# A hybrid decoder block on eight cores: norm sums of later first-FFN tiles placed behind their transfer, and a rebuilt last tile

## The chip, the cores and the metric

The kernel runs on the 8 cores of one Trainium2 chip. Each core computes one sequence of the batch, and no core talks to another. The time of a run is that of the slowest core, in microseconds (us). A profile is one further execution, recorded on every core; "the trace" below is that of core 7, the slowest, unless another core is named.

## The reference, cut to what matters

```python
def ada_rmsnorm(x, g, shift, scale):
    return rmsnorm(x, g) * (1.0 + scale[:, None, :]) + shift[:, None, :]
...
c_act = jax.nn.silu(c)
mod = c_act @ w_mod[l] + b_mod[l]                 # nine vectors of 1024
h = ada_rmsnorm(x, g_ffn1[l], sh1, sc1)
x = x + 0.5 * gt1[:, None, :] * swiglu_ffn(h, w_ffn1_in[l], w_ffn1_out[l])
h = ada_rmsnorm(x, g_mix[l], sh2, sc2)
...                                               # conv group and RG-LRU group, both from h @ w_in
x = x + gt2[:, None, :] * y_mix
h = ada_rmsnorm(x, g_ffn2[l], sh3, sc3)
x = x + 0.5 * gt3[:, None, :] * swiglu_ffn(h, w_ffn2_in[l], w_ffn2_out[l])
return ada_rmsnorm(x, g_final, f_shift, f_scale)
```

`x` is (8, 4096, 1024) in float32, the FFN's hidden width is 2816. Per core that is a first FFN, a mixer and a second FFN over 4096 tokens, with a norm over the 1024 channels ahead of each and one at the end.

## The kernel before

**Tiles.** The 4096 tokens are 8 tiles of 512. A tile of `x` lies in SBUF as 8 chunks (`fc` 0 to 7) of 128 channels x 512 tokens, so each channel sum of a norm runs across chunks and partitions: ScalarE squares a chunk, VectorE adds it to a running sum (`accum`), and after the eighth chunk one matmul with a matrix of ones (`total`) sums over the partitions into a PSUM bank. `rstd_ops` then takes Ln and Exp on ScalarE, and `apply` scales the chunks to bf16 in one of three buffers `hbs` (`sb_hb`). The running sum is `sb_rstdm`, the squares `sb_ntmp`, the last sum in bf16 `sb_sqb`; the final norm has its own, `sb_rstdo`, `sb_sqo`, `sb_sqbo`.

**Jobs.** `f_gen` runs the two FFNs over a ring of five weight slabs (`fslots`, `sb_fs`, 512 KB each), 33 slabs per job: 22 for the input matrix, 11 for the output matrix. The jobs are the first FFN of the pairs (2,3), (4,5), (0,1), then of tile 6, then the second FFN of 0 and 1, the first FFN of 7 and the second of 2 to 7. A slab of a pair feeds 32 matmuls, of a single tile 16. The next slab of the ring is asked for when one is free again. From tile 6 on the mixer of a tile (`r_gen`, `c_gen`, `mb_gen`) runs beside an FFN job. In the first jobs the float32 weights are also cast to bf16 copies in memory, and the modulation vectors are computed on VectorE from streamed `wmod`.

**Tiles of x.** There are four slots `xs` for tiles; slot 3 becomes mixer buffers after the pairs. `xl_gen` loads a tile of the input by eight transfers of 256 KB (`xload`, on POOL's queue). They share one semaphore, and `xload` gives every chunk the count and the planned time of the last one, so that whoever reads a chunk waits for the whole tile. `lx_gen` loads tiles 2 to 7 again from scratch memory for the mixer. A slot whose tile was written to `y` is loaded again with the next tile.

**The order of the work.** Nothing is ordered on the chip but by each engine's queue and its semaphores. The program is written out ahead: `run_streams` takes generators ("streams"), each of which yields an operation with a planned cost, and always emits the operation that could start first in planned time. Transfers have a planned landing time too, from a rate and a latency (`DMA_RATE`, `DMA_LAT`). Each engine then runs its list strictly in order. An operation that planned time puts ahead of a transfer's real landing therefore holds up everything behind it on its engine. `n1_gen` is the stream of the norms ahead of the first FFN. It takes an `hbs` buffer and the lock of the norm's buffers, and then yields the squares.

**The end of a tile.** `o_gen` does the final norm. It squares the chunks as the second FFN's output matmuls finish them (`x3c` flags), sums, then per chunk one VectorE multiply, one ScalarE Identity with the shift, and a 256 KB store to `y` on POOL's queue. Chunk `fc` of every tile uses semaphore `s_y[fc]`. After its last instruction POOL waits for all of them.

Every DMA, activation and vector operation is recorded by a helper, so rows name few lines: L417 the DMAs, L434 ScalarE, L437 and L441 VectorE, L457 matmuls.

## Time and profile before

| | |
|---|---|
| median of 3 runs | 2374.32 us (2369.19 to 2564.76) |
| the profiled execution, its own time | 2375.25 us |
| its span on core 7 (first to last instruction) | 2373.7 us |
| spans of all cores | 2348.4 to 2373.7 us |
| TensorE (PE) busy | 2249.8 us, 95% |
| VectorE (DVE) / ScalarE (ACT) / GpSimd (POOL) busy | 56% / 40% / 12% |
| granted TensorE clock, mean | 0.988 |

Times in rows are microseconds from the span's start. A row of a timeline has a start, a duration, the engine, the line, the operation, what it writes and reads, its count, and in brackets how long the engine was idle before it and what ended that. Rows of waits have the sum, the number and the longest. PEclk is the clock granted to TensorE, as a share of its 2.4 GHz. SPq and POOLq are the queues that issue transfers.

### The profile page before, as it was taken

How to read it: one execution, taken by the hardware profiler on the slowest of the kernel's cores; microseconds unless marked ns; L12 is line 12 of the kernel's file. 1: busy time of each engine (PE TensorE's matmuls, PEld its weight loads, DVE VectorE, ACT ScalarE, POOL GpSimd, SP SyncE). 2: the span in 40 equal slices, each digit the busy share in tenths (PEclk: the TensorE clock that was granted, in tenths of full speed). 3: DMA queues.
4: the chain of work that ended last, by engine and by line, in shares of the span. 5: the costliest groups of instructions: out<-in, count | busy, mean ns of one | idle time of the engine just before them, and what ended most of it. 6: DMA issues, size and time to landing. Idle time of an engine off the chain costs nothing.

```text
span 2373.7 us, 34088 instructions; the slowest of 8 cores (2348.4 to 2373.7 us)
## 1 busy us (share of the span) xinstructions
PE 2249.8 (95%) x10864; PEld 1006.1 (42%) x10864; DVE 1324.7 (56%) x2131; ACT 956.6 (40%) x1473; POOL 287.0 (12%) x552
## 2 busy tenths in 40 slices
PE   1999998998999899899999999999999999999995
PEld 0444443443444344344444444444444444444442
DVE  5323225524433485674776476487487588477522
ACT  3313213303110533553565536436536556454512
POOL 0011110020000110201110120111111111120000
PEclk9999999999999999999999999999999999999998
DMA  9899798899866685654665665556456566564452
GB/s 258 189 232 215 194 206 214 214 212 243 214 187 164 191 223 170 190 167 141 194 207 158 207 200 191 154 171 227 153 178 214 160 171 222 158 186 138 151 177 89
DMA packets 122704, 446.86 MB, mean 188 GB/s; under 512 B 18864, under 2 KB 19248, under 8 KB 121520
## 3 DMA queue, kind: packets, MB, share of 16 engines
q1 hardware_dynamic: 90864, 330.44, 44.7%
q0 software_dynamic: 31664, 114.23, 21.5%
q8 instruction: 91, 1.49, 0.3%
q14 instruction: 85, 0.70, 0.1%
HBM read 426.87 MB, written 71.30 MB: 210 GB/s over the span
## 4 chain that ended last, share of the span: by engine, by line
PE 85%; DMA 8%; issue 2%; DVE 2%; ACT 2%; POOL 1%; SPq 0%; DVEq 0%; ACTq 0%; POOLq 0%
PE ps L457 83%; DMA sb_x<-x 2%; PE ps L1097 2%; DMA sb_cs<-wmod 2%; DMA sb_fs<-b 1%; DMA sb_fs<-w 1%; DMA sb_hidB<-wmod 1%; DMA sb_cs<-bm 1%; DVE sb_rstdm L441 1%; DMA x<-sb_x 0%; SPq L417 0%; POOL sb_urep L1087 0%; ACT sb_hb L434 0%; POOL sb_x L417 0%; ACT sb_ntmp L434 0%
## 5 line engine op out<-in xcount | busy, mean ns | idle before, releaser
L457 PE MATMUL ps<-sb_hb,sb_fs 128*128 128x512 bf16 x5632 | 1245.6, 382 | 35.5 <-DMA sb_fs<-w 14.2
L457 PEld LDWEIGHTS ps<-sb_hb,sb_fs 128*128 128x128 bf16 x5632 | 553.9, 98 | 711.8 <-issue 62.5
L457 PE MATMUL ps<-sb_hidA,sb_fs 128*128 128x512 bf16 x2288 | 505.7, 379 | 0.8 <-DVE sb_hidA L441 0.8
L434 ACT ACTIVATE sb_sgf<-ps 128x512 f32<-128x512 f32 x352 | 206.5, 593 | 406.8 <-PE ps L457 364.3
L457 PEld LDWEIGHTS ps<-sb_hidA,sb_fs 128*128 128x128 bf16 x2288 | 223.9, 98 | 269.6 <-issue 1.3
L441 DVE TENSOR_TENSOR sb_hidA<-ps,sb_sgf 128x512 bf16<-128x512 f32 x286 | 195.4, 688 | 227.1 <-PE ps L457 161.4
L457 PE MATMUL ps<-sb_hb,sb_cs 128*128 128x512 bf16 x992 | 224.2, 379 | 4.5 <-DMA sb_cs<-bm 3.4
L1087 POOL DMA_DIRECT2D sb_urep<-sb_ub x256 | 131.0, 520 | 694.5 <-PE ps L457 435.6
L437 DVE SCALAR_TENSOR_TENSOR sb_x<-ps,sb_gth,sb_x 128x512 f32<-128x512 f32 x128 | 96.0, 750 | 174.8 <-PE ps L457 174.4
L434 ACT ACT_TABLE_LOAD x102 | 130.9, 1283 | 154.4 <-PE ps L457 134.1
L437 DVE SCALAR_TENSOR_TENSOR sb_ux<-sb_ub,sb_vecs,sb_ux 128x512 f32<-128x512 bf16 x240 | 179.7, 749 | 10.0 <-DVE sb_ux L437 0.9
L434 ACT ACTIVATE sb_ntmp<-sb_x 128x512 f32<-128x512 f32 x168 | 103.6, 627 | 197.7 <-DVE sb_x L437 110.7
L441 DVE TENSOR_TENSOR sb_rstdm<-sb_rstdm,sb_ntmp 128x512 f32<-128x512 f32 x144 | 99.3, 689 | 131.5 <-ACT sb_ntmp L434 127.5
L437 DVE SCALAR_TENSOR_TENSOR sb_ntmp<-sb_x,sb_gs,sb_rstdm 128x512 f32<-128x512 f32 x192 | 137.8, 748 | 50.0 <-ACT sb_rstdm L434 41.7
L434 ACT ACTIVATE sb_hb<-sb_ntmp,sb_modv 128x512 bf16<-128x512 f32 x192 | 133.1, 720 | 43.1 <-DVE sb_ntmp L437 42.7
L457 PEld LDWEIGHTS ps<-sb_hb,sb_cs 128*128 128x128 bf16 x992 | 96.5, 98 | 122.3 <-issue 7.6
L457 PE MATMUL ps<-sb_hb,sb_rs 128*128 128x512 bf16 x544 | 128.8, 381 | 0.6 <-DVE sb_gy L437 0.4
L457 PE MATMUL ps<-sb_hidB,sb_fs 128*128 128x512 bf16 x528 | 117.9, 379 | 0.0
L441 DVE TENSOR_TENSOR sb_hidB<-ps,sb_sgf 128x512 bf16<-128x512 f32 x66 | 45.6, 691 | 109.5 <-PE ps L457 106.0
L417 POOL DMA_DIRECT2D y<-sb_x x64 | 35.0, 547 | 521.3 <-ACT sb_sgf L434 198.0
L437 DVE SCALAR_TENSOR_TENSOR sb_x<-ps,sb_modv,sb_x 128x512 f32<-128x512 f32 x64 | 47.9, 749 | 74.4 <-PE ps L457 74.3
L457 PEld LDWEIGHTS ps<-sb_hb,sb_rs 128*128 128x128 bf16 x544 | 53.4, 99 | 66.7 <-issue 4.1
(104 smaller groups left out, 1338.6 us busy)
## 6 DMA issues: line engine op xcount, KB each, us to landing
sb_fs<-b SPq DMA_DIRECT2D x396, 512.0 KB, 4.4
sb_cs<-bm SPq DMA_DIRECT2D x78, 512.0 KB, 4.1
sb_x<-x POOLq DMA_DIRECT2D x96, 256.0 KB, 7.9
sb_cs<-wmod SPq DMA_DIRECT2D x46, 512.0 KB, 12.6
sb_rs<-bm SPq DMA_DIRECT2D x34, 512.0 KB, 5.0
sb_fs<-w POOLq DMA_DIRECT2D x33, 512.0 KB, 9.9
b<-sb_fs SPq DMA_DIRECT2D x33, 512.0 KB, 8.8
b<-w POOLq DMA_DIRECT2D x33, 512.0 KB, 10.3
```

What stands on the lines that cost most here:

```text
L417: return Op(eng, lambda h: [h.dma_start(out=out_ap, in_=in_ap)], reads, writes, dma=sem, nbytes=nbytes)
L434: return Op(ACT, lambda h: [h.activation(out=out, in_=in_, func=func, **kw)], reads, writes, cost, tset)
L437: return Op(DVE, lambda h: [h.scalar_tensor_tensor(out=out, in0=in0, scalar=scalar, in1=in1, op0=op0, op1=op1)], reads, writes, cost)
L441: return Op(DVE, lambda h: [h.tensor_tensor(out=out, in0=in0, in1=in1, op=op)], reads, writes, cost)
L457: out.append(h.matmul(ps[:, bank, :], lhsT=l, rhs=r, start=(first and k == 0), stop=(last and k == n - 1)))
L1087: out.append(h.dma_start(out=urep[q][32 * sft:32 * sft + 32, 1 - h2:2, :], in_=ub[32 * q:32 * q + 32, 1 + h2:2 * h2 + 2, sft:sft + WU]))
L1097: out.append(h.matmul(ps[32 * q:32 * q + 32, b, :], lhsT=sl[:, 8 * (c % 2) + r, 32 * q:32 * q + 32], rhs=urep[q][:, c % 2, 4 * r:4 * r + T ...
```

## The change

- **A planner condition for the norms of later first-FFN tiles.** `n1_gen` yields `landed(si, margin)` for every group but the first: the stream goes on once PE's planned clock is `margin` past the planned landing of the tile, 30 us for tiles 4, 5, 0 and 1, 12 us for 6 and 7. It stands ahead of the taking of `normlock`, behind that of the `hbs` buffer. It adds no instruction and no wait; it moves the norm's instructions in the lists. Should no stream have anything to emit, `core.force` lets all such conditions pass once.
- **Semaphores of the stores.** `s_y` is now one of four by tile (`t % 4`), shared by the tile's eight stores, and after the loop every chunk of the slot is marked with the full count. A later load into the slot waits for that.
- **The last tile** (`last`): the PSUM bank is taken at its start. Ahead of chunk 7's flag the ones matmul over the sum of chunks 0 to 6 is emitted (it opens the accumulation), and an Exp of one column (`hstate` into `sgm`), which brings the table load with it. Chunk 7's square is written as bf16 into `cvb` and summed by a second ones matmul into the same bank, in place of the last VectorE add. Its eight stores go from SyncE (`SP`) on a semaphore of their own, `s_yl`.
- **A renaming of the conv code** by the constants `CVD` and `CVP` (`spread`, `v_gen`, `c_gen`, the layout of `vecs`). With the values given it yields the same operations with the same operands.

```diff
@@ Core, run_streams
-        self.now = 0.0
+        self.force = False
...
-        assert best is not None, [s.name for s in streams]
+        if best is None:
+            assert not core.force, [s.name for s in streams]
+            core.force = True
+            continue
+        core.force = False
@@ semaphores
-        s_y = [newsem(f"s_y{k}") for k in range(8)]
+        s_y = [newsem(f"s_y{k}") for k in range(4)]
+        s_yl = newsem("s_yl")
@@ accum
-        def accum(st, src, r_src):
+        def accum(st, src, r_src, split=False):
...
+            if split and k == 7:
+                yield act(cvb[:], src, AF.Square, [r_src], [r_cvb])
+                return
             q = nxt(name, 2)
             yield act(sq[q][:], src, AF.Square, [r_src], [r_sq[q]])
-            if k < 7:
+            if split and k == 6:
+                yield add(accb[:], acc[:], sq[q][:], [r_sq[q], r_acc], [r_accb])
+            elif k < 7:
                 yield add(acc[:], acc[:], sq[q][:], [r_sq[q]], [r_acc])
@@ n1_gen
+        def landed(si, margin):
+            return lambda: core.force or PE.clock > max([r.tw for r in r_x[si]]) + margin
...
-                    yield lambda: normlock.take(1)
                     if first:
                         yield lambda: mused[0] >= 5
+                    elif gi > 0:
+                        yield landed(si, 30.0 if gi < 3 else 12.0)
+                    yield lambda: normlock.take(1)
@@ o_gen
-                yield from stats(xt, r_xt, st, before=lambda fc, t=t: flag(("x3c", t, fc)))
-                got = yield lambda: bankM.take(1)
-                bank = got[0]
-                yield total(st, bank)
+                last = t == n_tiles - 1
+                if last:
+                    got = yield lambda: bankM.take(1)
+                    bank = got[0]
+                    for fc in range(8):
+                        if fc == 7:
+                            yield mm(bank, [(ones_bf[:], sqbo[:])], [r_sqbo, r_ones], last=False)
+                            yield act(sgm[:, 0:1], hstate[:, 0:1], AF.Exp, [r_hst[0]], [r_sgm], tset="E", cost=0.2)
+                        yield flag(("x3c", t, fc))
+                        yield from accum(st, xt[:, fc, :], r_xt[fc], True)
+                    yield mm(bank, [(ones_bf[:], cvb[:])], [r_cvb, r_ones], first=False)
+                else:
+                    (the four lines removed above)
...
-                    yield dma(PL, y_d[t, fc], xt[:, fc, :], [r_xt[fc]], [], s_y[fc], MB // 4)
+                    sy = s_y[t % 4] if not last else s_yl
+                    yield dma(SP if last else PL, y_d[t, fc], xt[:, fc, :], [r_xt[fc]], [], sy, MB // 4)
+                for fc in range(8):
+                    r_xt[fc].r[sy] = sy.val
                 xpool.give(si)
```

POOL's final wait covers `s_y` and `s_yl`.

## Rows read from the trace of the kernel before

**Rows 1.** The page: the span, and busy time by engine.

```profile
span 2373.7 us, 34088 instructions; the slowest of 8 cores (2348.4 to 2373.7 us)
...
PE 2249.8 (95%) x10864; PEld 1006.1 (42%) x10864; DVE 1324.7 (56%) x2131; ACT 956.6 (40%) x1473; POOL 287.0 (12%) x552
```

**Rows 2.** Waits of PE over the whole span: total, times, longest.

```profile
PE ps L457 <- DVE sb_sqb L441: 56.1, 9, 33.0
```

**Rows 3.** Timeline of PE around the ones matmuls of tiles 0 and 6.

```profile
365.48 0.58 PE L457 MATMUL ps<-sb_sqb,sb_ones 128*128 128x512 bf16 x1 [5.96 <-DVE sb_sqb L441]
365.86 14.33 PE L457 MATMUL ps<-sb_hb,sb_fs 128*128 128x512 bf16 x55
...
540.61 22.57 PE L457 MATMUL ps<-sb_hb,sb_fs 128*128 128x512 bf16 x96 [2.87 <-DMA sb_fs<-b]
569.30 0.59 PE L457 MATMUL ps<-sb_sqb,sb_ones 128*128 128x512 bf16 x1 [6.13 <-DVE sb_sqb L441]
569.68 10.49 PE L457 MATMUL ps<-sb_hb,sb_fs 128*128 128x512 bf16 x35
```

**Rows 4.** Timeline of ACT: the first squares of tiles 0 and 6.

```profile
356.15 0.63 ACT L434 ACTIVATE sb_rstdm<-sb_x 128x512 f32<-128x512 f32 x1 [11.37 <-DMA sb_x<-x]
...
559.50 0.63 ACT L434 ACTIVATE sb_rstdm<-sb_x 128x512 f32<-128x512 f32 x1 [7.61 <-DMA sb_x<-x]
```

**Rows 5.** Stretches: length, busy PE, PEld, DVE, ACT, POOL (instructions), PEclk, DMA share, GB/s.

```profile
360.00:370.00 10.00, 4.52 (x11) 1.61 (x12) 6.96 (x13) 6.39 (x9) 0.00 (x0) 0.68 0.87 272
...
440.00:500.00 60.00, 60.00 (x279) 27.20 (x278) 26.22 (x40) 13.81 (x21) 7.51 (x14) 1.00 0.82 188
...
570.00:580.00 10.00, 10.00 (x35) 4.00 (x34) 7.06 (x12) 9.05 (x13) 0.00 (x0) 0.74 0.73 143
```

**Rows 6.** Slabs asked for at 530.92 and at 549.45: KB, us to landing.

```profile
sb_fs<-b SPq DMA_DIRECT2D x1, 512.0 KB, 34.2
...
sb_fs<-b SPq DMA_DIRECT2D x1, 512.0 KB, 30.7
```

**Rows 7.** Waits of PE on core 4, 340 to 600 us.

```profile
PE ps L457 <- DVE sb_sqb L441: 13.2, 2, 10.1
```

**Rows 8.** Timeline of PE: the ones matmul of tile 7's first norm.

```profile
1218.37 0.38 PE L457 MATMUL ps<-sb_sqb,sb_ones 128*128 128x512 bf16 x1 [1.02 <-DVE sb_ub L449]
```

**Rows 9.** Timeline of ACT: tile 5's first square, and the instruction after its norm.

```profile
232.40 0.63 ACT L434 ACTIVATE sb_rstdm<-sb_x 128x512 f32<-128x512 f32 x1 [22.57 <-DMA sb_x<-x]
...
288.80 1.28 ACT L434 ACT_TABLE_LOAD   x1 [34.67 <-PE ps L457]
```

**Rows 10.** Loads behind stores: waits for `y` by line, then the refill at 1642 us.

```profile
  POOL sb_x L417: 4.9, 4
...
1641.96 3.76 POOL L417 DMA_DIRECT2D sb_x<-x  x7
1647.38 0.54 POOL L417 DMA_DIRECT2D sb_x<-x  x1 [1.65 <-DMA y<-sb_x]
...
1656.26 0.63 ACT L434 ACTIVATE sb_rstdm<-sb_x 128x512 f32<-128x512 f32 x1 [2.37 <-DMA sb_x<-x]
```

**Rows 11.** Timeline of the last tile's final norm.

```profile
2350.75 0.69 DVE L441 TENSOR_TENSOR sb_sqbo<-sb_rstdo,sb_sqo 128x512 bf16<-128x512 f32 x1 [0.95 <-ACT sb_sqo L434]
...
2351.59 0.38 PE L457 MATMUL ps<-sb_sqbo,sb_ones 128*128 128x512 bf16 x1 [2.65 <-DVE sb_sqbo L441]
2352.10 1.28 ACT L434 ACT_TABLE_LOAD   x1 [1.52 <-PE ps L457]
...
2356.94 5.18 POOL L417 DMA_DIRECT2D y<-sb_x  x8 [99.19 <-ACT sb_x L434]
```

**Rows 12.** The stretch behind the last store, columns as in rows 5.

```profile
2365.00:2373.70 8.70, 0.00 (x0) 0.00 (x0) 0.00 (x0) 0.00 (x0) 0.00 (x0) 0.50 0.00 0
```

**Rows 13.** Timeline of ACT: a mixer's Exp and Ln operations behind one table load.

```profile
1014.71 1.28 ACT L434 ACT_TABLE_LOAD   x1
...
1018.85 2.18 ACT L434 ACTIVATE sb_mbuf<-sb_mbuf 128x512 f32<-128x512 f32 x4
```

More of the change, by code:

```diff
@@ L24 @@
 WU = 540
+CVD = (0,)
+CVP = (1, 2, 3)
 V_G1, V_GM, V_G2, V_GF = 0, 8, 16, 24
@@ L1082, in spread @@
         def spread(h2):
+            c0 = max(2 * h2, CVP[0])
             def fn(h):
@@ L1086, in fn @@
                     for sft in range(4):
-                        out.append(h.dma_start(out=urep[q][32 * sft:32 * sft + 32, 1 - h2:2, :],
-                                               in_=ub[32 * q:32 * q + 32, 1 + h2:2 * h2 + 2, sft:sft + WU]))
+                        out.append(h.dma_start(out=urep[q][32 * sft:32 * sft + 32, c0 - 2 * h2:2, :],
+                                               in_=ub[32 * q:32 * q + 32, c0:2 * h2 + 2, sft:sft + WU]))
                 return out
-            return Op(PL, fn, [r_ub[2 * h2 + k] for k in range(1 - h2, 2)], [r_urep], dma=s_ur, nbytes=128 * 4 * (1 + h2) * WU * 2, ndma=16)
+            return Op(PL, fn, [r_ub[k] for k in range(c0, 2 * h2 + 2)], [r_urep], dma=s_ur, nbytes=128 * 4 * (2 * h2 + 2 - c0) * WU * 2, ndma=16)
         def conv_mm(b, sl, r_sl, c):
@@ L1127, in c_gen @@
                 bankM.give(bv)
-                if c == 0:
-                    streams.append(Stream(f"V{i}", v_gen(i), dict(b_m, dve=0)))
-                if c == 1:
+                if c in CVD:
+                    streams.append(Stream(f"V{i}.{c}", v_gen(i, c), b_v))
+                if c == 1 and CVP[0] < 2:
                     yield spread(0)
             flags.add(("glu", i))
-            for c in range(1, 4):
+            for c in CVP:
+                if c == 2 and CVP[0] == 2:
+                    yield cring.has(k0 + 4)
+                    cring.done(k0 + 4)
+                    yield spread(1)
                 k = k0 + 4 + c // 2
@@ L1149, in c_gen @@
             cx = [ux[:, c, 3:3 + T] for c in range(4)]
-            yield act(varb[:], cx[1], AF.Square, [r_ux[1]], [r_var])
-            for c in (2, 3, 0):
-                if c == 2:
-                    yield add(meanb[:], cx[1], cx[2], [r_ux[1], r_ux[2]], [r_mean])
-                elif c == 3:
-                    yield add(meanb[:], meanb[:], cx[3], [r_ux[3]], [r_mean])
-                else:
-                    yield flag(("cv", i))
-                    yield add(cvb[:], meanb[:], cx[0], [r_ux[0], r_mean], [r_cvb])
+            lo = CVP + CVD
+            for n, c in enumerate(lo):
+                if c in CVD:
+                    yield flag(("cv", i, c))
+                if n == 0:
+                    yield act(varb[:], cx[c], AF.Square, [r_ux[c]], [r_var])
+                    continue
+                if n == 1:
+                    yield add(meanb[:], cx[lo[0]], cx[c], [r_ux[lo[0]], r_ux[c]], [r_mean])
+                elif n == 2:
+                    yield add(meanb[:], meanb[:], cx[c], [r_ux[c]], [r_mean])
+                else:
+                    yield add(cvb[:], meanb[:], cx[c], [r_ux[c], r_mean], [r_cvb])
                 yield act(sgm[:], cx[c], AF.Square, [r_ux[c]], [r_sgm])
-                if c > 0:
+                if n < 3:
                     yield add(varb[:], varb[:], sgm[:], [r_sgm], [r_var])
@@ L1273, in o_gen @@
                 st = stat_o()
-                yield from stats(xt, r_xt, st, before=lambda fc, t=t: flag(("x3c", t, fc)))
-                got = yield lambda: bankM.take(1)
-                bank = got[0]
-                yield total(st, bank)
+                last = t == n_tiles - 1
[10 more added lines that the diff above has]
+                else:
+                    yield from stats(xt, r_xt, st, before=lambda fc, t=t: flag(("x3c", t, fc)))
+                    got = yield lambda: bankM.take(1)
+                    bank = got[0]
+                    yield total(st, bank)
                 yield rstd_ops(rstd_o, r_ro, bank, 1.0 / D)
@@ L1316, in build_program @@
         build_program.model = {e.name: (round(e.clock, 1), round(e.busy, 1)) for e in (PE, ACT, DVE, SP, PL)}
-        final_vals = [(sm.h, sm.val) for sm in s_y]
+        final_vals = [(sm.h, sm.val) for sm in s_y + [s_yl]]
         with nc.Block() as block:
@@ L1367, in prep_inputs @@
             shared[:, V_RCW + 4 * cc + k] = rcw[k, cc * 128:(cc + 1) * 128]
-    shared[:, V_CW:V_CW + NCONV] = f(inputs["conv_w"][0])[:, 0:128].T
+    for j, cc in enumerate(CVD):
+        shared[:, V_CW + NCONV * j:V_CW + NCONV * (j + 1)] = f(inputs["conv_w"][0])[:, 128 * cc:128 * cc + 128].T
     def blocks(w, rows, cols):
```

20 lines of the change are left out of this document (11 added, 9 removed).

## Prediction

> **What bounds the kernel now.** I read the page first, then the waits of PE, then its timeline. PE is busy for 2249.8 of 2373.7 us, every other engine for at most 56% [rows 1]. So time is gained only where PE stands still, or behind its last matmul. The waits of PE say where it stands: 56.1 us in 9 waits are for `sb_sqb`, the last sum of a norm, that is, for a ones matmul which sits in PE's queue ahead of its data [rows 2]. The longest, 33.0 us, is the kernel's start, which the change does not touch. Of the rest, the timeline shows two large ones, 5.96 us at tile 0's norm and 6.13 us at tile 6's [rows 3]; the other 11.0 us are spread over six. The reader should follow each one step back. ACT stood for 11.37 and 7.61 us at the tile's first square, waiting for the transfer of `x` [rows 4]. The squares start when the tile lands, at 356.15 and 559.50; eight squares and seven adds later the sum is there, about 9 us on. PE had arrived at its ones matmul at 359.5 and 563.2. The planner had the tile land earlier than it did.
>
> **What a stall costs.** It is more than its idle time. Behind the first, 55 matmuls take 14.33 us [rows 3]; at the full clock they take 0.215 us each (60.00 us for 279 in [rows 5]), 11.83 in all. The granted clock of that stretch is 0.68, so part of it ran at 1.2 instead of 2.4 GHz [rows 5]. That is 2.5 us more, and the first stall costs 5.96 + 2.50 = 8.5 us. Behind the second, 35 matmuls take 10.49 us in place of 7.53, at a granted clock of 0.74 [rows 3, 5]: 6.13 + 2.96 = 9.1 us.
>
> **The norms moved back.** Nothing is added; the squares, adds, ones matmul, Ln, Exp and the 16 operations of `apply` go later in three queues. The first stall: PE came 6 us early, the margin is 30. It goes whole, 8.5 us. Nothing is late next: the pair (4,5) began at about 287 us (its first Silu stands behind ACT's table load at 288.80 [rows 9]) and takes 33 slabs of 32 x 0.215 = 6.9 us, so tile 0 is wanted from about 515 on. Does the gain survive until then? The weights must come as much earlier. Between 440 and 500 us the DMA engines are busy for a share of 0.82 [rows 5], so 0.18 x 60 = 11 us are spare, more than 8.5. I keep it all.
>
> The second stall: PE was 6 us early, the margin is 12, so the sum is ready first. But here the weights come next. PE had just done 96 matmuls, three slabs of the pair, behind a wait of 2.87 us for a slab [rows 3], so slabs come with nothing to spare. The one it takes next was asked for at 530.92 and took 34.2 us [rows 6]: it landed at 565.1, and 1.9 us of the stall stay. The slab two further on was asked for at 549.45 and took 30.7 us, landing at 580.15; with 6.9 us for a pair's slab (32 x 0.215) PE wants it at 565.1 + 13.8 = 578.9 and waits 1.2 us more. From then on PE is at 580.15 where it was 64 matmuls behind 569.68: 35 in 10.49 us, 29 more in 6.2, at 586.4. The gain is 6.2 us, between 3.5 (if these slabs get no sooner and a clock drop follows their wait) and 9.1 (if the transfers move up with PE).
>
> Tiles 4 and 1 show no wait of PE and give nothing. Tile 5's squares started at 232.40, its norm left ACT at 288.80 - 34.67 = 254.1, and ACT's next work comes at 288.8 [rows 9]. Thirty us later it ends at 284.1, so 4.7 us of cover are left; without them tile 4 alone could run up to the ring's five slabs ahead, 17 us. Nothing. Tile 7's ones matmul comes 1.02 us late [rows 8]: 1.0 us gained, between 0 and 2.
>
> **The stores' semaphores.** Before, a load into a freed slot waited for its own chunk's store. At 1641.96 POOL issued seven of the eight loads while the last store was still under way, and only the eighth waited, until 1647.38 [rows 10]. After the change all eight wait, so the last is issued 7 x 0.54 = 3.8 us later, and what stands behind them on POOL's queue (the 16 transfers of a `urep` spread, the stores of `y`, tile writes) is as late at most. Such waits for `y` occur four times [rows 10]. How much later does the tile land? Nothing, if the eight loads are limited by their 2 MB (the last one took until 1656.26, 8.9 us behind its issue); 3.8 us, if by their issue. I take the middle, 1.9. One of the four is tile 7's first load, where the margin of 12 us covers it. At 1656.26 ACT already waits 2.37 us for the tile [rows 10], so the 1.9 us may reach PE there. For the other two, which no large wait of PE marks (they are among the six that share 11.0 us), I take 0.6 together. Loss 2.5 us, between 0 and 8 (3.8 at two of them).
>
> **The last tile.** The last VectorE add goes. Its row starts at 2350.75 and the ones matmul at 2351.59 [rows 11], 0.84 us; the second ones matmul starts as soon as the square is there. The table load of 1.28 us stands between that matmul and Ln [rows 11]; moved ahead, it lies beside PE's last eight matmuls (8 x 0.215 = 1.7 us), for which chunk 7's square waits anyway. The stores: ACT is done at 2361.0, POOL's last issue starts 0.54 before 2362.12, at 2361.58 [rows 11], since POOL spends 0.54 to 0.66 us on each. SyncE has nothing else to do then: 0.5 us, perhaps 0.7 with a shorter way to the data, between 0 and 1.3. The added ones matmul costs 0.2 us of PE ahead of the end, the Exp of one column nothing. Together 0.84 + 1.28 + 0.7 = 2.8 us, between 1.9 and 3.4.
>
> The Trainium skill's page "ScalarE: Activation LUTs" (section "What ACT_TABLE_LOAD costs") gives about 2.66 us for a switch of tables, load and drain together. By it the last tile would save 1.4 us more. The trace doesn't agree: the instruction behind the load starts 1.29 us after the load did.
>
> **Sum.** 8.5 + 6.2 + 1.0 + 2.8 - 2.5 = 16.0 us. The profiled execution took 2375.25 us (span 2373.7 and 1.5 around it), so 2359.2 us; it lies 0.9 above the median of the runs shown. I predict **2358 us**. Other cores have the same stalls; core 4 loses 13.2 us in two of them [rows 7], so the slowest core should gain about as much as core 7.
>
> **Rivals.**
> - *The transfers become the bound.* PE's wait for a slab at 540.6 (2.87 us, [rows 3]) grows by what the first stall gave: the queue that took 34.2 us for a slab [rows 6] is no faster. Then 8.5 us are given back at about 540 us: gain 7.5, **2367 us**. For it: landing times of over 30 us. Against: the spare 11 us at 440 to 500 us. Chance 0.17.
> - *A new order brings new waits.* The planner rebuilds every queue from the first moved norm on, and what waits remain (the 11.0 us in six for `sb_sqb` among them, [rows 2, 3]) falls by chance. Two new ones of 8 us undo the change: **2374 us**. The trace can't price this. Chance 0.13.
> - *The other side: refills.* Each of the four refills is 3.8 us late and drops the clock for 2.5 us as the stalls did, 25.2 in all, against 18.5 gained: **2381 us**. It decides from 4.6 us per refill. Against: tile 7's is covered, and at the one in [rows 10] PE lost no more than its share of 11.0 us though the tile was 2.37 us late for ACT. Chance 0.05.
> - *The condition is too weak for tile 6.* It counts in planned time. Core 4's longest stall is 10.1 us [rows 7], the margin 12. If the tile comes 4 us later still, the second gain is lost: **2364 us**. Chance 0.05.
> - *The end shrinks.* For 8.7 us behind the last store no engine works and nothing moves [rows 12]. If that is POOL's closing of its own transfers, it could fall away with stores on SyncE: **2350 us**. But POOL still waits for the stores and has issued transfers all along. Chance 0.07.
> - *The table load stays.* If an Exp ahead brings a table without Ln, a second load follows: 1.3 us more, **2360 us**. Against: in the mixer one load covers four Exp, two Ln and two Exp, with the Exp first [rows 13]. Chance 0.02. The Trainium skill's page "ScalarE: Activation LUTs" (section "Table sets: the hidden batching unit") lists a set for Exp that lacks Ln beside one that has both; by that rule the load would stay if the first were picked.
>
> **How the numbers follow.** The forecast has the other 0.51. Forecast, too-weak condition, staying load, transfers and shrinking end hold 0.82; with the bounds of the small terms that is 2349 to 2369 us. The measurement can tell about 2%, here 47 us, from no change. No case reaches that on either side: faster 0.02, within 2% 0.96, slower 0.02, the two for what I have not thought of.
>
> **What would show it.** Right: no wait of PE over 1 us at the ones matmuls of tiles 0 and 6, and the granted clock 1.00 behind them; a slab wait of 1 to 3 us at about 555 us; the eight loads of a refill in one run behind the last store's landing; at the end no table load between ones matmul and Ln, and the last store issued 0.1 us behind the last Identity; 8.7 us of quiet at the end as before. Wrong: waits for slabs of over 8 us more than before, ones matmuls that wait in the mixer part, or a tile 4/5 job that starts with one tile only.

## The result, and the profile after

The changed kernel is slightly slower. Over 20 runs each its median is 2398.91 us against 2378.72 us; the ratio is 1.0067, with a 95% interval of 1.0047 to 1.0087, so about 16 us were lost (11 to 21) where 16 were forecast as a gain. (The medians count every run; the ratios, here and below, leave out the disturbed ones.) The profiled execution took 2381.32 us, the quickest of its 20; before it was 2375.25 us.

The page of the changed kernel, to be held against [rows 1]:

```profile
span 2379.7 us, 34056 instructions; the slowest of 8 cores (2365.9 to 2379.7 us)
PE 2253.4 (95%) x10865; PEld 1007.1 (42%) x10865; DVE 1322.6 (56%) x2130; ACT 953.5 (40%) x1472; POOL 282.8 (12%) x544
```

The work is the same to one matmul, and PE is no less the bound. So the loss, like the hoped-for gain, lies in PE's waits. Its waits over the whole span on core 1, which answer to [rows 2]:

```profile
PE ps L464 <- DVE sb_sqb L448: 63.4, 9, 32.3
```

The start still holds 32.3 us; the other eight waits for a norm's sum add up to 31.1 us on this core, where on core 7, the slowest of the kernel before, they were 23.1. (All helper lines moved by seven: L457 is now L464, L441 is L448, L434 is L441, L417 is L424.)

**Where tile 0's norm waits now.** The timeline of core 1 around it (start, length, engine, line, operation, in brackets the idle time ahead and what ended it):

```profile
374.71 1.22 DVE L663 SCALAR_TENSOR_TENSOR sb_junk<-sb_cs,sb_cb 128x1024 bf16<-128x1024 f32 x1 [7.01 <-DMA sb_cs<-wmod]
...
376.64 0.60 ACT L441 ACTIVATE sb_sgf<-ps 128x512 f32<-128x512 f32 x1 [8.25 <-DVE sb_hidA L448]
377.13 0.62 ACT L441 ACTIVATE sb_rstdm<-sb_x 128x512 f32<-128x512 f32 x1
...
385.71 1.22 DVE L663 SCALAR_TENSOR_TENSOR sb_junk<-sb_cs,sb_cb 128x1024 bf16<-128x1024 f32 x1 [8.57 <-DMA sb_cs<-wmod]
...
387.47 2.27 DVE L448 TENSOR_TENSOR sb_rstdm<-sb_rstdm,sb_ntmp 128x512 f32<-128x512 f32 x3
388.24 0.63 ACT L441 ACTIVATE sb_ntmp<-sb_x 128x512 f32<-128x512 f32 x1 [8.96 <-DVE sb_rstdm L448]
...
393.57 0.59 PE L464 MATMUL ps<-sb_sqb,sb_ones 128*128 128x512 bf16 x1 [13.06 <-DVE sb_sqb L448]
```

Read the lines in order of time. ACT's first square, at 377.13, waits for nothing any more: the tile has long landed, and the 11.37 us of [rows 4] are gone. But VectorE, which must add the squares, stands in its own queue at a product of the modulation, the multiply of a `wmod` slab (`sb_junk`, L663). Two such slabs are late: VectorE stands 7.01 and 8.57 us for them. The adds stand behind them, ACT's squares behind the adds, and PE's ones matmul comes 13.06 us late, where it had been 5.96 [rows 3]. This is not peculiar to core 1: on core 7, the slowest of the kernel before, it is 8.28 us.

The stretch of the stall and the one behind it, on core 1, columns as in [rows 5]:

```profile
380.00:390.00 10.00, 0.52 (x3) 0.02 (x1) 4.08 (x7) 1.43 (x3) 0.00 (x0) 0.77 0.98 311
390.00:400.00 10.00, 6.42 (x18) 2.43 (x19) 7.25 (x12) 7.78 (x11) 0.00 (x0) 0.55 0.23 90
```

In the second stretch the granted clock is 0.55, nearly the lower level of 1.2 GHz throughout. While PE stood, the DMA engines were busy for a share of 0.98; behind the stall it is 0.23. So the transfers already asked for ran on beside the stall, and then few were under way. That new ones waited for buffers that PE and VectorE had to free would explain it; no run tests that.

Tile 6's stall shrank on five of the eight cores and grew on three. On core 7 it was 6.13 us [rows 3] and is 1.47, on core 1 it is 2.43; the mean over the cores went from 6.1 to 4.2. On core 5 it went from 4.94 to 10.76 us, by the same mechanism as at tile 0:

```profile
555.62 0.63 ACT L441 ACTIVATE sb_rstdm<-sb_x 128x512 f32<-128x512 f32 x1 [3.46 <-DMA sb_x<-x]
563.65 1.23 DVE L663 SCALAR_TENSOR_TENSOR sb_junk<-sb_cs,sb_cb 128x1024 bf16<-128x1024 f32 x1 [11.40 <-DMA sb_cs<-wmod]
571.11 0.59 PE L464 MATMUL ps<-sb_sqb,sb_ones 128*128 128x512 bf16 x1 [10.76 <-DVE sb_sqb L448]
```

Here ACT still waits for the tile too, 3.46 us (1.3 to 3.5 us on four cores), so the 12 us of planned margin are not always enough.

**Where a refill waits now.** The timeline of core 7 around 1640 us, the same core and refill as in [rows 10]:

```profile
1640.76 0.54 POOL L424 DMA_DIRECT2D y<-sb_x  x1 [3.76 <-ACT sb_varb L441]
1646.52 4.24 POOL L424 DMA_DIRECT2D sb_x<-x  x8 [5.22 <-DMA y<-sb_x]
1659.66 0.63 ACT L441 ACTIVATE sb_rstdm<-sb_x 128x512 f32<-128x512 f32 x1 [6.50 <-DMA sb_x<-x]
1667.43 0.50 PE L464 MATMUL ps<-sb_sqb,sb_ones 128*128 128x512 bf16 x1 [4.68 <-DVE sb_sqb L448]
```

In the kernel before, the last store was issued at 1641.43 and the first of the eight loads at once behind it, at 1641.96. Now all eight stand until that store has landed, 5.22 us. ACT's wait for the tile grew from 2.37 to 6.50 us and PE's from 0.67 to 4.68. POOL's waits for `y`, 4.9 us in 4 [rows 10], are now, on the same core:

```profile
POOL sb_x L424 <- DMA y<-sb_x: 23.9, 5, 5.4
```

**The end** is the part that did what it should. The timeline of core 1 from the table load on:

```profile
2354.78 1.28 ACT L441 ACT_TABLE_LOAD   x1
...
2356.07 0.20 ACT L441 ACTIVATE sb_sgm<-sb_hstate 128x1 f32<-128x1 f32 x1
...
2359.81 0.38 PE L464 MATMUL ps<-sb_cvb,sb_ones 128*128 128x512 bf16 x1 [1.73 <-ACT sb_cvb L441]
2360.28 0.60 ACT L441 ACTIVATE sb_rstdo<-ps 128x512 f32<-128x512 f32 x1 [0.62 <-PE ps L464]
...
2363.65 4.85 SPq L424 DMA_DIRECT2D y<-sb_x  x8
```

The table load stands ahead, no second one follows between the ones matmul and Ln, and the stores leave from SyncE's queue. From the start of the last ones matmul to the end of the span it is 19.9 us, where it was 22.1 (2351.59 in [rows 11] to 2373.7); from the end of the last matmul of the second FFN it is 21.5 in place of 24.8 us in the mean over the cores, 3.3 us less.

**A ledger.** For every kernel below: PE's waits in three stretches (340 to 600 us, 600 to 1190, 1190 to 2100), for all releasers together, then the time from the last ones matmul to the end of the span, then the mean span. All are means over the eight cores of the profiled execution. The last column is the ratio of the timed runs to the kernel before, timed beside them, with its 95% interval; it rests on 13 runs of the changed kernel and on 5 to 11 of each other, on 5 for the shared semaphores alone, the products 20 us behind and the margin of 12.

| kernel | 340-600 | 600-1190 | 1190-2100 | end | mean span | ratio |
|---|---|---|---|---|---|---|
| before | 14.4 | 15.6 | 8.4 | 22.1 | 2361.6 | |
| after | 18.3 | 17.3 | 15.7 | 19.8 | 2373.6 | 1.0067 [1.0047, 1.0087] |
| shared semaphores alone | 13.1 | 17.4 | 20.9 | 22.7 | 2380.3 | 1.0058 [1.0046, 1.0071] |
| condition alone | 18.2 | 17.3 | 7.1 | 22.1 | 2365.9 | 1.0002 [0.9990, 1.0015] |
| last tile alone | 15.0 | 17.7 | 8.7 | 19.7 | 2360.0 | 0.9978 [0.9965, 0.9992] |
| after, a semaphore for each chunk | 19.4 | 16.8 | 6.3 | 19.2 | 2361.5 | 0.9983 [0.9974, 0.9993] |
| two semaphores for each tile | 13.8 | 15.1 | 9.7 | 23.1 | 2362.1 | 1.0002 [0.9983, 1.0021] |
| products 20 us behind their slab | 7.8 | 18.4 | 6.9 | 19.2 | 2350.5 | 0.9919 [0.9892, 0.9947] |
| final wait on SyncE | 17.2 | 14.9 | 6.7 | 11.3 | 2347.8 | 0.9964 [0.9941, 0.9986] |
| margin 12 for all | 10.6 | 17.7 | 6.2 | 19.2 | 2351.3 | 0.9952 [0.9930, 0.9974] |
| all good parts | 6.2 | 18.5 | 7.0 | 11.3 | 2339.8 | 0.9915 [0.9887, 0.9943] |
| before, products 20 us behind | 12.1 | 18.3 | 8.8 | 22.6 | 2361.6 | 1.0022 [0.9993, 1.0052] |

For the change: 3.9 + 1.7 + 7.3 us more of waits, 2.3 less at the end, 10.6 in all, of the 12.0 us by which the mean span grew. Ahead of 340 us, outside the table, the waits are 1.1 us less (49.7 against 50.8). What is left may be the lower granted clock behind the longer waits; it was not measured by itself. One trace of a kernel also differs from another's where no edit reaches: the kernel with the last tile alone has 2.1 us more of waits than before between 600 and 1190 us. So 1.7 us there say nothing about the norms; the 7.3 us are well above that.

### The profile page after: what moved, and what is told of

It reads as the page before. It is cut to its first block, busy times and chain, and to the rows that moved or that the text cites. A ratio compares the mean times of both kernels' runs of the same rounds, so it can differ in the third digit from the quotient of the medians.

```text
span 2379.7 us, 34056 instructions; the slowest of 8 cores (2365.9 to 2379.7 us)
## 1 busy us (share of the span) xinstructions
PE 2253.4 (95%) x10865; PEld 1007.1 (42%) x10865; DVE 1322.6 (56%) x2130; ACT 953.5 (40%) x1472; POOL 282.8 (12%) x544
## 3 DMA queue, kind: packets, MB, share of 16 engines
q0 software_dynamic: 31024, 112.13, 21.5%
## 4 chain that ended last, share of the span: by engine, by line
PE 83%; DMA 9%; ACT 2%; DVE 2%; issue 2%; POOL 1%; SPq 0%; DVEq 0%; ACTq 0%; POOLq 0%
PE ps L464 81%; DMA sb_cs<-wmod 3%; DMA sb_x<-x 2%; PE ps L1116 2%; DMA sb_fs<-b 2%; DVE sb_rstdm L448 1%; POOL sb_x L424 1%; DMA y<-sb_x 1%; DMA sb_fs<-w 0%; DMA x<-sb_x 0%; ACT sb_sgf L441 0%; ACT L441 0%; ACT sb_x L441 0%; ACT sb_ntmp L441 0%; DMA sb_cs<-bm 0%
## 5 line engine op out<-in xcount | busy, mean ns | idle before, releaser
L464 PE MATMUL ps<-sb_hb,sb_fs 128*128 128x512 bf16 x5632 | 1249.6, 383 | 38.3 <-DMA sb_fs<-w 12.5
L464 PEld LDWEIGHTS ps<-sb_hb,sb_fs 128*128 128x128 bf16 x5632 | 554.8, 99 | 717.9 <-issue 70.8
L464 PE MATMUL ps<-sb_hidA,sb_fs 128*128 128x512 bf16 x2288 | 505.7, 379 | 1.0 <-DVE sb_hidA L448 1.0
L441 ACT ACTIVATE sb_sgf<-ps 128x512 f32<-128x512 f32 x352 | 206.2, 592 | 440.1 <-PE ps L464 368.2
L464 PEld LDWEIGHTS ps<-sb_hidA,sb_fs 128*128 128x128 bf16 x2288 | 223.8, 98 | 270.1 <-issue 1.9
L448 DVE TENSOR_TENSOR sb_hidA<-ps,sb_sgf 128x512 bf16<-128x512 f32 x286 | 195.1, 687 | 232.5 <-PE ps L464 158.6
L464 PE MATMUL ps<-sb_hb,sb_cs 128*128 128x512 bf16 x992 | 224.2, 379 | 1.7 <-DMA sb_cs<-bm 1.7
L441 ACT ACTIVATE sb_ntmp<-sb_x 128x512 f32<-128x512 f32 x168 | 103.5, 626 | 229.0 <-DVE sb_rstdm L448 117.0
L448 DVE TENSOR_TENSOR sb_rstdm<-sb_rstdm,sb_ntmp 128x512 f32<-128x512 f32 x144 | 99.2, 689 | 122.6 <-ACT sb_ntmp L441 118.1
L441 ACT ACTIVATE sb_hb<-sb_ntmp,sb_modv 128x512 bf16<-128x512 f32 x192 | 133.5, 718 | 46.0 <-DVE sb_ntmp L444 45.6
L464 PEld LDWEIGHTS ps<-sb_hb,sb_cs 128*128 128x128 bf16 x992 | 96.6, 98 | 119.3 <-issue 4.6
L464 PE MATMUL ps<-sb_hb,sb_rs 128*128 128x512 bf16 x544 | 128.8, 381 | 0.4 <-DVE sb_gy L444 0.4
L464 PE MATMUL ps<-sb_hidB,sb_fs 128*128 128x512 bf16 x528 | 118.2, 379 | 0.0
L448 DVE TENSOR_TENSOR sb_hidB<-ps,sb_sgf 128x512 bf16<-128x512 f32 x66 | 45.5, 690 | 103.8 <-PE ps L464 99.0
L663 DVE SCALAR_TENSOR_TENSOR sb_junk<-sb_cs,sb_cb 128x1024 bf16<-128x1024 f32 x46 | 56.1, 1219 | 47.7 <-DMA sb_cs<-wmod 47.3
L464 PEld LDWEIGHTS ps<-sb_hb,sb_rs 128*128 128x128 bf16 x544 | 53.3, 98 | 66.0 <-issue 3.0
```

The costliest lines, as they stand in the source:

```text
L441: return Op(ACT, lambda h: [h.activation(out=out, in_=in_, func=func, **kw)], reads, writes, cost, tset)
L448: return Op(DVE, lambda h: [h.tensor_tensor(out=out, in0=in0, in1=in1, op=op)], reads, writes, cost)
L464: out.append(h.matmul(ps[:, bank, :], lhsT=l, rhs=r, start=(first and k == 0), stop=(last and k == n - 1)))
L663: yield Op(DVE, lambda h, ap=ap, b=b: [h.scalar_tensor_tensor(out=junk[:], in0=ap, scalar=1.0, in1=cb[:], op0=ALU.mult, op1=ALU.mult, accu ...
```

## Which part of the change did it

Three kernels make one part of the change each. They, and all kernels below that are called the kernel before with some edit, keep the renamed conv code; ratios of 1.0002 for two of them show that it costs nothing that can be measured. The first has only the shared semaphores for the stores; the program lists the same instructions in the same order as before.

```diff
-        s_y = [newsem(f"s_y{k}") for k in range(8)]
+        s_y = [newsem(f"s_y{k}") for k in range(4)]
...
-                    sy = s_y[fc]
+                    sy = s_y[t % 4]
...
+                for fc in range(8):
+                    r_xt[fc].r[sy] = sy.val
```

> The kernel before with one edit: the eight stores of a tile share one semaphore, and a load into the slot waits for all eight. Every engine's list of instructions is that of before. Theory A (the shared semaphore is what made the whole change slower): a refill's last load is issued some 4 us later, the ones matmuls at about 1334, 1469 and 1664 us wait 2 to 5 us longer than before, one wait at about 2000 us is new, and the kernel is 8 to 14 us slower than before (+0.35 to +0.6%). Rival B (the moved norms did it): no more than 3 us slower.

Measured: ratio 1.0058 [1.0046, 1.0071], 13.8 us more (10.9 to 16.9). The ledger has most of it in one place: 12.5 us more of waits between 1190 and 2100 us, where the refills are. Of these 7.3 are waits for a norm's sum: at the second of the five refills behind stores, near 1330 us, PE's wait goes from 0 to 3.4 us in the mean over the cores, at the third, near 1660, from 0.9 to 4.4. About 5 more stand near 1200 and 2000 us, beside the first refill and the last, as waits for `sb_hidA` and `sb_sgf`; what ties them to the refills stays open. The wait near 1469, expected to grow too, is at a load behind no store of `y`, and hardly moved (2.8 to 3.2). The third refill on core 5:

```profile
1650.07 0.54 POOL L424 DMA_DIRECT2D y<-sb_x  x1 [3.75 <-ACT sb_varb L441]
...
1655.44 4.24 POOL L424 DMA_DIRECT2D sb_x<-x  x8 [4.83 <-DMA y<-sb_x]
...
1670.19 0.63 ACT L441 ACTIVATE sb_rstdm<-sb_x 128x512 f32<-128x512 f32 x1 [7.73 <-DMA sb_x<-x]
...
1678.02 0.59 PE L464 MATMUL ps<-sb_sqb,sb_ones 128*128 128x512 bf16 x1 [5.97 <-DVE sb_sqb L448]
```

From the first load's issue to the tile's first square it is 14.75 us; in [rows 10] it is 14.30 (1641.96 to 1656.26). There the last of the eight was issued 5.4 us behind the first, here 3.7 us. So the tile lands about as long behind the *first* issue as before, though the last one follows it sooner, and the wait for the last store is passed on: ACT's wait is 5.4 us longer than in [rows 10]. Core 5 is the extreme. In the mean over the cores the first load of this refill is issued 4.5 us later, and 3.5 us of that reach the tile (13.6 in place of 14.6 us from first issue to first square).

The second kernel has only the planner's condition.

```diff
-                    yield lambda: normlock.take(1)
                     if first:
                         yield lambda: mused[0] >= 5
+                    elif gi > 0:
+                        yield landed(si, 30.0 if gi < 3 else 12.0)
+                    yield lambda: normlock.take(1)
```

> The kernel before with the planner's condition alone (30 and 12 us behind the landing). Theory A: tile 6's stall goes, tile 0's comes back at about 390 us since VectorE waits there for a late slab of modulation weights ahead of the norm's adds, so between 5 us faster and 4 us slower than before. Rival B (the moved norms made the whole change slower): 8 us slower or more.

Measured: ratio 1.0002 [0.9990, 1.0015]. No gain. The norm of tile 0 stalls on every core, for 6.0 to 12.8 us, and the ledger has 18.2 us of waits between 340 and 600 us where before it was 14.4. On core 5:

```profile
376.82 1.22 DVE L663 SCALAR_TENSOR_TENSOR sb_junk<-sb_cs,sb_cb 128x1024 bf16<-128x1024 f32 x1 [10.30 <-DMA sb_cs<-wmod]
...
384.68 0.59 PE L464 MATMUL ps<-sb_sqb,sb_ones 128*128 128x512 bf16 x1 [6.95 <-DVE sb_sqb L448]
385.06 13.30 PE L464 MATMUL ps<-sb_hb,sb_fs 128*128 128x512 bf16 x49
```

VectorE waits 10.30 us for its slab, the sum is late, and the 49 matmuls behind take 13.30 us, where 49 x 0.215 = 10.5 us would do at the full clock.

The third has only the last tile's edits.

```diff
+                        if fc == 7:
+                            yield mm(bank, [(ones_bf[:], sqbo[:])], [r_sqbo, r_ones], last=False)
+                            yield act(sgm[:, 0:1], hstate[:, 0:1], AF.Exp, [r_hst[0]], [r_sgm], tset="E", cost=0.2)
...
+                    yield dma(SP if last else PL, y_d[t, fc], xt[:, fc, :], [r_xt[fc]], [], sy, MB // 4)
```

> The kernel before with the rebuilt last tile alone. Both theories: about 3 us faster than before (-0.13%), which the measurement hardly tells from nothing; in the profile 24.7 us from PE's last FFN matmul to the end of the span become about 21.6.

Measured: ratio 0.9978 [0.9965, 0.9992], 5 us less (2 to 8). The trace shows 2.4 us less from the last ones matmul on and 3.3 us less from the last matmul of the second FFN on; 0.65 us of both are a shorter close of GpSimd, of which more below. The forecast's 2.8 us fit the second figure and the timed runs.

The fourth is the whole change with a store semaphore for each chunk, as before.

```diff
-                    sy = s_y[t % 4] if not last else s_yl
+                    sy = s_y[fc] if not last else s_yl
...
-                for fc in range(8):
-                    r_xt[fc].r[sy] = sy.val
```

> The kernel after with the semaphores of the stores as before (one per chunk). Theory A: the waits at the refills fall back to those of before, and the time is 8 to 14 us under that of the kernel after, so from 2 us above to 8 us below the kernel before. Rival B: as slow as the kernel after, 10 us or more above before.

Measured: ratio 0.9983 [0.9974, 0.9993], 4 us less than before and some 20 us less than the whole change. So the shared semaphores alone turn a small gain into a loss. The parts add up to 13.8 + 0.5 - 5.2 = 9.1 us, the whole change has 15.9; the intervals (about 4 to 14, and 11 to 21) overlap. Whether the semaphores cost more in the new order than in the old one is not settled.

## Is it the first load's wait or the last one's?

The prediction had the last of the eight loads in view. To tell the two apart, each tile got two semaphores, one for chunks 0 to 3 and one for 4 to 7. The first load waits for the fourth store, long landed; the last four still stand until the last store is there. Against the kernel with the shared semaphores alone:

```diff
-        s_y = [newsem(f"s_y{k}") for k in range(4)]
+        s_y = [newsem(f"s_y{k}") for k in range(8)]
...
-                    sy = s_y[t % 4] if not last else s_yl
+                    sy = s_y[2 * (t % 4) + fc // 4] if not last else s_yl
...
                 for fc in range(8):
+                    sy = s_y[2 * (t % 4) + fc // 4] if not last else s_yl
                     r_xt[fc].r[sy] = sy.val
```

> The kernel before, with two semaphores per tile for its stores: chunks 0 to 3 share one, chunks 4 to 7 the other; a load waits for its own half. Theory A (what costs is that the FIRST load of a refill waits for the last store, since the eight loads take some 14 us from their first issue on): now the first four loads wait only for stores that have long landed, so within 2 us of before. Rival C (what costs is the LAST load's issue): four loads still follow the last store's landing, 1.6 us instead of 3.8 us later than before, so about 5 us slower.

Measured: ratio 1.0002 [0.9983, 1.0021], so the 13.8 us are gone but for at most 5. The refill on core 7:

```profile
1640.11 0.54 POOL L424 DMA_DIRECT2D y<-sb_x  x1 [3.76 <-ACT sb_varb L441]
1640.64 2.13 POOL L424 DMA_DIRECT2D sb_x<-x  x4
1645.52 2.12 POOL L424 DMA_DIRECT2D sb_x<-x  x4 [2.75 <-DMA y<-sb_x]
```

The last four begin 2.75 us late, and the tile's first square comes at 1654.28, 13.64 us behind the first issue. In the mean over the cores, for this refill:

| kernel | first load behind the last store's issue | last load behind it | first square behind the first load | PE's wait |
|---|---|---|---|---|
| before | 0.5 | 5.2 | 14.6 | 0.9 |
| one semaphore for each tile | 5.1 | 8.8 | 13.6 | 4.4 |
| two for each tile | 0.5 | 6.7 | 14.4 | 0.8 |

With two semaphores the last load is issued 1.5 us later than before, and the tile lands no later; with one it is 3.6 us later, and the tile 3.5. One semaphore alone would fit the last load as the cause as well as the first. Two decide it: had the last load set the landing, PE's wait would have grown and not stayed at 0.8 us. The timed runs by themselves would still allow the 5 us that were expected for the last load, just at the interval's end. It is the first load's wait that costs.

The Trainium skill's page "DMA: Bandwidth & Descriptors" (section "Why a DMA increments its semaphore by 16 and not by 1") states that an intermediate count doesn't say which of several transfers on a shared semaphore has landed. This is why a shared one must be waited for in full; no run here tests that, only what the full wait costs a refill.

## Is it the modulation's slabs?

The condition counts from the landing of `x` alone. The next kernel is the fourth one (the whole change with a store semaphore for each chunk) with one number changed: the planner puts a product of the modulation 20 us in place of 8 us behind its slab's planned landing.

```diff
-                    yield lambda: PE.clock > r_ms[k % NM].tw + 8.0 or fring.freed >= 3 * NF1 - 2
+                    yield lambda: PE.clock > r_ms[k % NM].tw + 20.0 or fring.freed >= 3 * NF1 - 2
```

> The kernel after without the shared semaphores, and the modulation products on VectorE planned 20 us behind their slab's planned landing in place of 8. Theory A (the stall at tile 0's norm is now VectorE's wait for a late modulation slab, ahead of the norm's adds): the wait of PE at about 390 us, 7 to 14 us before, falls under 3 us, and the time is 5 to 10 us under that of the kernel after without the shared semaphores. Rival D (the moved norm's squares and adds themselves come too late): the wait stays.

Measured: ratio 0.9919 [0.9892, 0.9947], 19 us less than before, and 15 less than the fourth kernel. Both stalls are gone on all eight cores (no wait for `sb_sqb` over 0.3 us between 340 and 600 us). PE's timeline on core 1:

```profile
371.71 7.72 PE L464 MATMUL ps<-sb_hb,sb_fs 128*128 128x512 bf16 x35
379.49 0.38 PE L464 MATMUL ps<-sb_sqb,sb_ones 128*128 128x512 bf16 x1
379.70 20.67 PE L464 MATMUL ps<-sb_hb,sb_fs 128*128 128x512 bf16 x95
...
537.44 22.82 PE L464 MATMUL ps<-sb_hb,sb_fs 128*128 128x512 bf16 x93 [6.61 <-DMA sb_fs<-b]
...
567.64 0.38 PE L464 MATMUL ps<-sb_sqb,sb_ones 128*128 128x512 bf16 x1
```

The ones matmul passes between full-speed matmuls. VectorE's waits for slabs on this core between 340 and 600 us, above those in the changed kernel and below in this one:

```profile
DVE sb_junk L663 <- DMA sb_cs<-wmod: 38.0, 9, 9.7
DVE sb_junk L663 <- DMA sb_rs<-wmod: 36.7, 6, 13.0
```

```profile
DVE sb_junk L663 <- DMA sb_cs<-wmod: 7.2, 3, 3.9
```

At 537.44 stands the wait of which the first rival spoke, for a slab of the pair. PE's waits for such slabs between 340 and 600 us are 7.0 us in the mean over the cores, against 2.7 before. So the transfers do take back part of what the norms give, 4.3 us, not 8.5. The timed runs gain 19 us (13 to 26), the mean span of the one trace 11.1.

**The same number in the kernel before.** If the modulation's slabs were the whole cause, the condition would not be needed.

```diff
-                    yield lambda: PE.clock > r_ms[k % NM].tw + 8.0 or fring.freed >= 3 * NF1 - 2
+                    yield lambda: PE.clock > r_ms[k % NM].tw + 20.0 or fring.freed >= 3 * NF1 - 2
```

> The kernel before with one edit: the modulation products on VectorE are planned 20 us behind their slab instead of 8. Theory A (two late transfers stand behind one stall, x for ScalarE and modulation for VectorE; both must be cleared): ScalarE still waits for x at tiles 0 and 6, PE still loses 4 to 7 us at each, and the kernel gains at most 6 us. Rival E (the modulation slabs were the whole cause from the start): 12 us or more under before, and the stalls at 365 and 569 us are gone.

Measured: ratio 1.0022 [0.9993, 1.0052]. No gain, and PE still waits 7.1 to 11.9 us per core for the two norms (9.0 to 13.2 before). On core 1 the first one still begins late for its tile:

```profile
350.74 0.63 ACT L441 ACTIVATE sb_rstdm<-sb_x 128x512 f32<-128x512 f32 x1 [8.79 <-DMA sb_x<-x]
...
361.21 0.38 PE L464 MATMUL ps<-sb_sqb,sb_ones 128*128 128x512 bf16 x1 [2.81 <-DVE sb_sqb L448]
```

So two late transfers stand behind one stall. `x` came first in the kernel before and hid the other; each edit alone gives nothing (1.0002 and 1.0022), both together 14 us (0.9919, against 0.9978 with the last tile's edits alone, each within 0.003; 9.5 us by the mean spans). At tile 6 the other was not even hidden. On core 7 of the kernel before, the same product stands between that tile's first square, at 559.50 [rows 4], and its adds:

```profile
561.44 1.23 DVE L656 SCALAR_TENSOR_TENSOR sb_junk<-sb_cs,sb_cb 128x1024 bf16<-128x1024 f32 x1 [6.11 <-DMA sb_cs<-wmod]
```

**A smaller margin.** A rival was that the 30 us are themselves at fault, since they put the norm among slabs that are later still.

```diff
-                        yield landed(si, 30.0 if gi < 3 else 12.0)
+                        yield landed(si, 12.0)
```

> The kernel after without the shared semaphores, with a margin of 12 us for all later tiles, so that tile 0's norm lies some 18 us earlier than with 30. Theory A (what counts is what VectorE waits for at that place, not how far the norm is behind its transfer): the stall at tile 0's norm changes in size without a rule, between 0 and 13 us; time within 6 us of the kernel with 30. Rival D (a larger margin is simply too late): the stall is under 2 us.

Measured: ratio 0.9952 [0.9930, 0.9974], between the fourth kernel and the one with 20 us. PE's wait for the norms' sums between 340 and 600 us is anything from 0.7 to 14.1 us, by the core; it was 11.6 to 18.4 with 30 us. The place matters, but a margin on `x` alone leaves to chance what VectorE's queue then waits for.

## What stands at the end

For 8.7 us behind the last store no engine worked [rows 12]. In the traces of before and after it is the same: once POOL's wait for the stores is over, GpSimd's closing DRAIN takes 8.56 us on each core, to the second decimal, and the span ends 0.23 us behind it. In the other kernels in which POOL waits last it is between 7.91 and 9.54 us, and again the same on all eight cores: 0.65 us shorter where the last tile's eight stores leave from SyncE, 0.65 longer with one semaphore for each tile, 0.98 with two. Why is open; it accounts for most of the differences between 22.1, 22.7 and 23.1 in the ledger's column "end". The next kernel is the fourth one, with the wait for the stores at the end of SyncE's program in place of POOL's, so that POOL can close when its own last transfer is out.

```diff
             def _(h):
                 replay(SP, h)
+                for smh, v in final_vals:
+                    if v:
+                        h.wait_ge(smh, v)
...
             def _(h):
                 replay(PL, h)
-                for smh, v in final_vals:
-                    if v:
-                        h.wait_ge(smh, v)
```

> The kernel after without the shared semaphores, and the wait for all stores of y at the program's end moved from GpSimd to SyncE. If the 8.6 us behind the last landing are GpSimd's own closing, which starts when its wait is over, it now runs beside the last tile: 8 to 9 us under the kernel after without the shared semaphores. If they belong to the end of any program: no change.

Measured: the DRAIN takes 8.8 to 9.7 us (7.91 in the fourth kernel), but it starts some 100 us before the end, beside matmuls. The end behind the last ones matmul is 11.2 to 11.4 us on all cores, where the fourth kernel has 19.1 to 19.4. The last rows of core 0, whose span is 2367.5 us:

```profile
2356.23 0.38 PE L464 MATMUL ps<-sb_cvb,sb_ones 128*128 128x512 bf16 x1 [1.73 <-ACT sb_cvb L441]
...
2360.08 4.71 SPq L424 DMA_DIRECT2D y<-sb_x  x8
```

The ratio is 0.9964 [0.9941, 0.9986], 4.5 us under the fourth kernel's; the two intervals reach 5 and 2 us to either side and overlap, so the timed runs alone don't prove the 7.9 us that every core's trace shows.

The Trainium skill's page "VectorE: DVE Perf Modes" (section "The DRAIN you can't avoid") puts the DRAINs of a kernel's start and end at about 12 ns, on all engines. If GpSimd's last one is to be counted among them, this case's traces don't agree: it takes 7.91 us or more in each.

**All good parts together**: the changed kernel without the shared semaphores, with products 20 us behind their slab, and the final wait on SyncE.

```diff
-                    yield lambda: PE.clock > r_ms[k % NM].tw + 8.0 or fring.freed >= 3 * NF1 - 2
+                    yield lambda: PE.clock > r_ms[k % NM].tw + 20.0 or fring.freed >= 3 * NF1 - 2
...
+                for smh, v in final_vals:
+                    if v:
+                        h.wait_ge(smh, v)
```

> The kernel after without the shared semaphores, with the modulation products 20 us behind their slabs and the final wait on SyncE. If the gains add (19 us and 8.5 us, in different places): about 2350 us, 1.1 to 1.3% under before.

Measured: median 2353.44 us against 2374.07, ratio 0.9915 [0.9887, 0.9943], 20 us less (14 to 27). It beats both kernels. It was expected to gain about 8 us over the one with the slabs' margin alone. Its mean span is 10.7 us shorter, but the ratios (0.9915 and 0.9919, each within 0.0028) don't tell the two apart.

## Why the prediction was wrong, step by step

**"It goes whole, 8.5 us" (the first stall).** This is the step that failed first. The prediction followed the stall back to ACT's wait for `x` [rows 4] and stopped there. It asked what PE would miss next, the weights, and found cover; it did not ask what the moved instructions would stand behind on the two other engines. VectorE's queue holds products of the modulation whose slabs VectorE waits 7 to 11 us for, and the adds now come behind them: the stall went from 4.8 to 9.3 us in the mean over the cores. With those products later, the stall does go. Held against before, with the last tile's edits taken off, both edits give 14 us by the timed runs and 9.5 by the mean spans, where the prediction had 8.5 + 6.2 = 14.7 for the two stalls. So the size of the stalls was about right, the cover was not. The spare transfer time was read too narrowly as well: the share of 0.82 is that of 440 to 500 us, and between 500 and 560 us the trace of before has 0.97 to 1.03, also on core 7.

**"6.2 us" (the second stall).** On core 7 the stall itself went from 6.13 to 1.47 us. But the slab waits foreseen there, 1.9 + 1.2 us, came as 3.41 and 2.37:

```profile
569.01 8.47 PE L464 MATMUL ps<-sb_hb,sb_fs 128*128 128x512 bf16 x32 [3.41 <-DMA sb_fs<-b]
578.95 0.38 PE L464 MATMUL ps<-sb_sqb,sb_ones 128*128 128x512 bf16 x1 [1.47 <-DVE sb_sqb L448]
581.70 18.68 PE L464 MATMUL ps<-sb_hb,sb_fs 128*128 128x512 bf16 x78 [2.37 <-DMA sb_fs<-b]
```

With the slab wait of [rows 3], 2.87 us before and 0.62 after, PE's waits for slabs and the norm went from 9.0 to 7.9 us there: 1.1 us of waits gained, below the bound of 3.5. On the other cores single slab waits are anything from 0.2 to 5.6 us, and where both edits are made a longer one stands at 537 on core 1 (6.61). The next limit was the right one and was put too low. In the mean over the cores 4.2 us of the stall are left, and the rival "the condition is too weak for tile 6" has its part in that: on four cores ACT still waits for the tile. With both edits the stall is gone. The sum's 1.0 us at tile 7 came: that ones matmul waits no more.

**"Loss 2.5 us, between 0 and 8" (the stores' semaphores).** Measured alone, 13.8 us (10.9 to 16.9), outside the term's own bounds. Both ends of that range were worked out from how late the *last* of eight loads is issued. The row showed seven loads issued ahead of the last store's landing [rows 10], so the first one was about to lose 5 us, and nothing was made of it. One semaphore for each tile costs 13.8 us, two for each tile nothing that can be measured.

**The rival "refills"** had the mechanism and put its point of decision at 4.6 us per refill; POOL's five waits are 2.6 to 7.9 us, by refill and core. It got 0.05; against it was said that PE lost little there before. PE lost little (0.67 us on core 7) because the tile was just in time; a tile that is just in time passes on nearly every further us, and that should have spoken for the rival. Its price, four times 3.8 us and a drop of the clock, came out at 25.2 us, too much: in the changed kernel two of the refills reach PE's wait for the norm, by 3.5 and 3.8 us more in the mean over the cores (0 to 3.5 near 1330 us, 0.9 to 4.7 near 1660).

**"2.8 us" (the last tile).** Right, and in the foreseen form: 3.3 us in the trace from the last FFN matmul on, 5 us (2 to 8) in the runs of that part alone. The table load stays ahead of Ln, so the rival that it returns didn't come true. The quiet at the end stayed, as was held against the rival "the end shrinks"; POOL's wait had to be moved as well, and then that rival's 8 us appear in every trace.

**"The transfers become the bound".** In part. It gives back 4.3 us where the stalls are gone; in the changed kernel itself PE's waits for slabs between 340 and 600 us are 3.8 us in the mean, against 2.7.

**"A new order brings new waits"** is closest to what happened to tile 0's norm, and had 0.13. But it was set down as chance that a trace can't price. It could have been priced: the late slabs were in the trace of before as VectorE's waits, up to 12.7 us between 340 and 600 us on core 7, and at tile 6 one stood within the norm itself (the row at 561.44 above).

**The sum.** In the ledger the terms of the change are: 3.9 us lost around the two norms where 15.7 were to be gained at the norms; refills 7.3 us lost (12.5 alone) where 2.5 were allowed; the end 2.3 gained where 2.8 were. The range of 2349 to 2369 us had no place for a wrong cover, since each rival took one failure at a time.

## What to carry to other kernels

When instructions are moved back to escape a late transfer, list everything that the queues of *all* engines involved wait for in the new place, and give each of them its margin; a stall behind which two transfers are late gives nothing until both are cleared. When semaphores are merged, look at the first instruction that waits, not the last: a refill here landed about as long behind its first issue whenever the last came, so a wait ahead of the first load is passed on nearly whole, while one in the middle of the loads was free here. Where an engine has closing work of its own, its last wait belongs on another engine.

## What the runs showed of the hardware

GpSimd's closing DRAIN, where it stands behind the final wait, is 8.56 us long in before and after and 7.91 to 9.54 us in the other kernels, the same on all eight cores of a kernel; beside other work, in the two kernels with the final wait on SyncE, it is 8.8 to 10.0 us, and hidden there.

Eight loads of 256 KB at the refill near 1640 us land 11.8 to 15.9 us behind the issue of the first one, by kernel and core. The kernel's mean is 14.6 us in before (the last issued 4.6 us behind the first), 13.6 with one semaphore for each tile (3.7) and 14.4 with two (6.1): the spread of the issues moves it by 1 us at most.

Waits of PE of 3.0 to 13 us had a lower clock behind them. Behind the wait of 13.06 us the granted clock of 10 us was 0.55; on core 1 of the changed kernel it was 0.83 behind waits of 4.22, 3.82 and 3.03 us, but 1.00 behind one of 2.43. Behind a wait of 6.95 us 49 matmuls took 13.30 in place of 10.5 us, 2.8 us on top of the wait, as both stalls of before had shown (2.5 and 2.96 us).
